# Hybrid encoder block on one core: four of twelve 128-column turns move from TensorE to VectorE blocks and transfers

## The reference

```python
h = rms_norm(x, g_mix);  proj = h @ w_in          # z | xbc | dt | q | k | v | gates
y = ssd_scan_both_ways(conv(xbc), dt) + d_skip * xs
y = rms_norm_by_group(y * silu(z)) * norm_g        # 8 groups of 256 channels
attn = gqa(rope(norm(q)), rope(norm(k)), v)
x = x + (sigmoid(ga) * (y @ w_ssm_up) + sigmoid(gb) * (attn @ w_attn_up)) @ w_out
x = x + relu(rms_norm(x) @ w_mlp_in)**2 @ w_mlp_out
out = rms_norm(x) * g_final
```

## Time and profile before

| | us |
|---|---|
| median of 3 runs (1622.29 to 1622.76) | 1622.51 |
| profiled execution, first to last instruction (its span) | 1620.0 |
| outside of the span, median less span | 2.5 |
| PE busy | 1608.5 (99%) |
| DVE busy | 1264.1 (78%) |
| ACT busy | 917.1 (57%) |

### The profile page before, as it was taken

One profiled execution on the slowest core, in us unless ns is written; L12 is line 12 of the kernel. 1 busy time (PEld: TensorE's weight loads), 2 busy tenths in 40 slices (PEclk: granted clock), 3 DMA queues, 4 the chain that ended last, 5 costly groups with the idle time before them and its releaser, 6 DMA issues.

```text
span 1620.0 us, 20751 instructions
## 1 busy us (share of the span) xinstructions
PE 1608.5 (99%) x8104; PEld 1362.2 (84%) x8104; DVE 1264.1 (78%) x1520; ACT 917.1 (57%) x1262; POOL 79.1 (5%) x67
## 2 busy tenths in 40 slices
PE   9999999999999999999999999999999999999998
PEld 7888888888888888888888888888888888888886
DVE  7888878888666677776665576999799988998893
ACT  6666556666565445544444555665556556655562
POOL 3000000000001134000000000000000000000000
PEclk9999999999999999999999999999999999999999
DMA  7666665666556664445576676458646764586471
GB/s 272 202 200 190 189 200 189 208 195 203 183 186 182 191 187 153 142 145 175 187 229 195 225 236 187 144 182 285 184 125 224 262 190 134 194 282 209 148 245 53
DMA packets 134194, 312.21 MB, mean 193 GB/s; under 512 B 9744, under 2 KB 10448, under 8 KB 133968
## 3 DMA queue, kind: packets, MB, share of 16 engines
q1 hardware_dynamic: 129376, 302.21, 58.4%
q10 hardware_dynamic: 4720, 8.68, 2.0%
HBM read 308.68 MB, written 2.16 MB: 192 GB/s over the span
## 4 chain that ended last, share of the span: by engine, by line
PE 96%; DVE 2%; issue 1%; ACT 0%; POOL 0%; DMA 0%; POOLq 0%; DVEq 0%
PE G L1719 17%; PE G L1720 17%; PE G L1721 17%; PE G L1728 13%; PE S L1728 7%; PE G L1732 6%; PE S L1719 4%; PE S L1721 4%; PE S L1720 4%; PE S L1732 4%; PE S L1740 1%; PE S L1847 1%; DVE wlo L1022 1%; PE S L1891 0%; PE S L1824 0%
## 5 line engine op out<-in xcount | busy, mean ns | idle before, releaser
L637 ACT ACTIVATE whi<-raw 128x1024 fp32r<-128x1024 f32 x395 | 417.0, 1059 | 418.1 <-PE G L1721 254.9
L1022 DVE TENSOR_TENSOR wlo<-raw,whi 128x1024 fp32r<-128x1024 f32 x395 | 482.5, 1236 | 128.7 <-ACT whi L637 127.4
L1719 PE MATMUL G<-whi,a_both 128*128 128x512 f32 x768 | 301.3, 392 | 2.3 <-DVE wlo L1022 1.7
L1721 PE MATMUL G<-whi,a_both 128*128 128x512 f32 x768 | 299.5, 390 | 0.0
L1720 PE MATMUL G<-wlo,a_both 128*128 128x512 f32 x768 | 299.5, 390 | 0.0
L1728 PE MATMUL G<-a_both,whi 128*128 128x512 f32 x640 | 201.7, 397 | 0.0
L1719 PEld LDWEIGHTS G<-whi,a_both 128*128 128x128 f32 x768 | 144.3, 188 | 33.3 <-issue 2.6
L1721 PEld LDWEIGHTS G<-whi,a_both 128*128 128x128 f32 x768 | 144.2, 188 | 30.1
L1720 PEld LDWEIGHTS G<-wlo,a_both 128*128 128x128 f32 x768 | 144.3, 188 | 28.7
L1732 PEld LDWEIGHTS G<-a_both,wlo 128*128 128x128 f32 x640 | 120.3, 188 | 28.2
L1719 PE MATMUL G<-whi,b_hi 128*128 128x512 f32 x342 | 133.9, 392 | 0.0
(11 more groups left out here) (306 smaller groups left out, 2692.4 us busy)
## 6 DMA issues: line engine op xcount, KB each, us to landing
raw<-in_w_in SPq DMA_DIRECT2D x208, 512.0 KB, 4.3
raw<-in_w_mlp_in SPq DMA_DIRECT2D x74, 512.0 KB, 4.0
raw<-in_w_mlp_out SPq DMA_DIRECT2D x74, 512.0 KB, 5.0
gates<-in_w_mlp_in SPq DMA_DIRECT2D x54, 512.0 KB, 4.0
gates<-in_w_mlp_out SPq DMA_DIRECT2D x54, 512.0 KB, 4.9
raw<-in_w_ssm_up SPq DMA_DIRECT2D x32, 512.0 KB, 3.8
raw<-in_w_attn_up SPq DMA_DIRECT2D x32, 512.0 KB, 4.6
raw<-in_w_out SPq DMA_DIRECT2D x32, 512.0 KB, 4.6
```

The lines of the kernel that those rows point to most:

```text
L637: act.activation(high(m), piece(n), ACT.Copy).then_inc(hi_made, 1)
L1022: dve.tensor_tensor(low(m), piece(n), high(m).bitcast(F32), ALU.subtract).then_inc(lo_made, 1)
L1719: pe.matmul(out_ap, hi[:, k, cols], w_hi, start=start, stop=False)
L1721: return pe.matmul(out_ap, lo[:, k, cols], w_hi, start=False, stop=stop)
```

## The change

Rounds 0 to 3 of the turning (the four parts of y) no longer use PE. Instead:

- zgate step 5, DVE: one `transpose` instruction turns each 32 by 32 block of `tmp_a` in place in the grid and writes `blocks` (128 partitions by 1024).
- zgate step 6, ACT: a transfer puts `blocks` into device memory, `block_rows`.
- next window, new side function `zturned`, step 0, ACT: waits until the transfer has landed, and issues four transfers that fetch the blocks to their places in `turned_to`; each goes to 32 partitions, in runs of 32 elements (128 bytes).
- step 3, ACT: waits for all four and writes `b_hi` from `turned_to`; step 4, DVE: writes `b_lo`.

`zturned(j)` stands ahead of `zgate(j + 1)`, and for j = 3 ahead of `rope(0)`. The buffers lie where the scan's tables were. Rounds 4 to 11 stay on PE; their code gains branches that are not taken, and two waits of PE on earlier rounds are placed a few steps apart from before.

```diff
 TS_Z, TS_MERGED, TS_X2, TS_END = 0, 4, 8, 12
+ON_PE = {rnd: i + 1 for i, rnd in enumerate((*range(TS_MERGED, TS_END),))}
+BLOCK_ROUNDS = [rnd for rnd in range(TS_END) if rnd not in ON_PE]
+Q = 32
...
-    window(9, 0, "z", 2, [("zgate", 1)])
-    window(9, 1, "z", 3, [("zgate", 2)])
-    window(10, 0, "k", 0, [("zgate", 3)])
-    window(10, 1, "v", 0, [("rope", 0)])
+    window(9, 0, "z", 2, [("zturned", 0), ("zgate", 1)])
+    window(9, 1, "z", 3, [("zturned", 1), ("zgate", 2)])
+    window(10, 0, "k", 0, [("zturned", 2), ("zgate", 3)])
+    window(10, 1, "v", 0, [("zturned", 3), ("rope", 0)])
...
+        def put_blocks(rnd):
+
+            d = BLOCK_ROUNDS.index(rnd)
+            act.wait_ge(blocks_turned, d + 1)
+            act.dma_start(block_rows[d], blocks[:, :, :].rearrange("p b n -> p (b n)")).then_inc(s_put, 16)
+
+        def get_blocks(rnd):
+
+            d = BLOCK_ROUNDS.index(rnd)
+            act.wait_ge(s_put, 16 * (d + 1))
+            if rnd:
+                act.wait_ge(ts_lo, rnd)
+            rows = block_rows[d].rearrange("(i r) (m j w) -> j r m i w", i=4, j=4, w=Q)
+            for j in range(4):
+                act.dma_start(turned_to[Q * j:Q * (j + 1), :, :].rearrange("r m (i w) -> r m i w", i=4), rows[j]
+                              ).then_inc(s_got, 16)
...
-            act.wait_ge(ts_t, rnd + 1)
+            if rnd in ON_PE:
+                act.wait_ge(ts_t, ON_PE[rnd])
+            else:
+                act.wait_ge(s_got, 64 * (BLOCK_ROUNDS.index(rnd) + 1))
...
-            if p == 7:
+            if p == 6:
+                put_blocks(TS_Z + j)
+
+        def zturned(p, j, pr, pp):
+            if p == 0:
+                get_blocks(TS_Z + j)
+            if p == 3:
                 split_high(TS_Z + j, b_hi, 4 * j, gain=2)
...
+        def turn_blocks(rnd, src):
+
+            d = BLOCK_ROUNDS.index(rnd)
+            if d:
+                dve.wait_ge(s_put, 16 * d)
+            dve.transpose(blocks[:, :, :].rearrange("p b n -> p (b n)").rearrange("p (c b t) -> p c b t", c=4, b=TB),
+                          src.rearrange("p b (c t) -> p c b t", c=4)).then_inc(blocks_turned, 1)
...
-            if p == 7:
+            if p == 5:
+                dve.wait_ge(z_v, (j + 1) * Z_V)
+                turn_blocks(TS_Z + j, tmp_a[:, :, :])
+
+        def zturned(p, j, pr, pp):
+            if p == 4:
                 split_low(TS_Z + j, b_hi, b_lo, 4 * j, gain=2)
...
-        def zgate(p, j, pr, pp):
-            if p == 6:
-                pe.wait_ge(z_v, (j + 1) * Z_V)
-                if j == 0:
-                    pe.wait_ge(scan_v, SCAN_V * GROUPS)
-                split_round(TS_Z + j, lambda c, tb: tmp_a[:, tb, c * P:(c + 1) * P])
-
```

More of the change, by code:

```diff
@@ L543, in build @@
     cum_rows = nc.dram_tensor("cum_rows", (2, HEADS, T), F32).ap()
+    block_rows = nc.dram_tensor("block_rows", (len(BLOCK_ROUNDS), P, TB * N), F32).ap()
+    by_channel = turned_to[:, :, :].rearrange("p (c b) t -> p c (b t)", b=TB)
     block = keep.enter_context(nc.Block())
@@ L654, in split @@
             high_part(m, n)
-        def split_high(rnd, dst, k0, gain=None, factor=1.0):
-            act.wait_ge(ts_t, rnd + 1)
+        def put_blocks(rnd):
[11 more added lines that the diff above has]
+                              ).then_inc(s_got, 16)
+        def split_high(rnd, dst, k0, gain=None, factor=1.0):
+            if rnd in ON_PE:
+                act.wait_ge(ts_t, ON_PE[rnd])
+            else:
+                act.wait_ge(s_got, 64 * (BLOCK_ROUNDS.index(rnd) + 1))
+                if gain is None:
+                    last = act.activation(dst[:, ds(k0, 4), :], by_channel,
+                                          ACT.Copy, scale=factor)
+                else:
+                    for c in range(4):
+                        last = act.activation(dst[:, k0 + c, :], by_channel[:, c, :],
+                                              ACT.Copy, scale=gains[:, gain * KT + k0 + c:gain * KT + k0 + c + 1])
+                last.then_inc(ts_hi, 1)
+                return
             if gain is None:
@@ L831, in zgate @@
                 if j:
-                    act.wait_ge(ts_t, TS_Z + j)
+                    act.wait_ge(blocks_turned, j)
                 else:
@@ L913, in merged @@
         def merged(p, j, pr, pp):
-            if p == 2:
+            if j + TS_MERGED not in ON_PE and p == 1:
+                put_blocks(j + TS_MERGED)
+            if j + TS_MERGED not in ON_PE and p == 3:
+                get_blocks(j + TS_MERGED)
+            if p == (2 if j + TS_MERGED in ON_PE else 6):
                 split_high(j + TS_MERGED, b_hi, j * 4, factor=0.5)
         def residual(p, j, pr, pp):
+            if TS_X2 + j not in ON_PE and p == 1:
+                put_blocks(TS_X2 + j)
+            if TS_X2 + j not in ON_PE and p == 3:
+                get_blocks(TS_X2 + j)
+            if p == (2 if TS_X2 + j in ON_PE else 6):
+                split_high(TS_X2 + j, a_hi, 4 * j, gain=1)
             if p == 2:
-                split_high(TS_X2 + j, a_hi, 4 * j, gain=1)
                 for tb in range(TB):
@@ L977, in finish @@
                     final_squares(j, tb)
-        table = {f.__name__: f for f in (rates, decays, conv, scan, gate, zgate, rope, values, attend, merged,
+        table = {f.__name__: f for f in (rates, decays, conv, scan, gate, zgate, zturned, rope, values, attend, merged,
                                          residual, hidden, finish)}
@@ L1052, in split @@
                 low_part(m, n + i - 3)
+        def turn_blocks(rnd, src):
[4 more added lines that the diff above has]
+                          src.rearrange("p b (c t) -> p c b t", c=4)).then_inc(blocks_turned, 1)
         def split_low(rnd, hi, lo, k0, gain=None, factor=1.0):
             dve.wait_ge(ts_hi, rnd + 1)
+            if rnd not in ON_PE:
+                if gain is None:
+                    part = slice(k0, k0 + 4)
+                    last = dve.scalar_tensor_tensor(
+                        out=lo[:, part, :], in0=by_channel, scalar=factor, in1=hi[:, part, :].bitcast(F32),
+                        op0=ALU.mult, op1=ALU.subtract)
+                else:
+                    for c in range(4):
+                        k = gain * KT + k0 + c
+                        last = dve.scalar_tensor_tensor(
+                            out=lo[:, k0 + c, :], in0=by_channel[:, c, :], scalar=gains[:, k:k + 1],
+                            in1=hi[:, k0 + c, :].bitcast(F32),
+                            op0=ALU.mult, op1=ALU.subtract)
+                last.then_inc(ts_lo, 1)
+                return
             if gain is None:
@@ L1456, in residual @@
                 add_product(j, pr, pp, lambda tb: out_product(j, tb))
-            if p == 2:
+                if TS_X2 + j not in ON_PE:
+                    dve.wait_ge(taken[pp], pr + 1)
+                    turn_blocks(TS_X2 + j, x_sb[:, j, :, :])
+            if p == (2 if TS_X2 + j in ON_PE else 7):
                 split_low(TS_X2 + j, a_hi, a_lo, 4 * j, gain=1)
@@ L1571, in finish @@
                     times_gain(j, tb)
-        table = {f.__name__: f for f in (rates, decays, conv, scan, tables, zgate, rope, attend, gated_a, merged,
+        table = {f.__name__: f for f in (rates, decays, conv, scan, tables, zgate, zturned, rope, attend, gated_a, merged,
                                          residual, hidden, sums, mixed, mix_out, finish)}
@@ L1912, in merged @@
         def merged(p, j, pr, pp):
-            if p == 1:
+            if p == 1 and j + TS_MERGED in ON_PE:
                 pe.wait_ge(merge_v, j + 1)
@@ L1918, in residual @@
         def residual(p, j, pr, pp):
-            if p == 1:
+            if p == 1 and TS_X2 + j in ON_PE:
                 pe.wait_ge(taken[pp], pr + 1)
@@ L1928, in residual @@
                 last.then_inc(row_mm, 1)
-        table = {f.__name__: f for f in (rates, decays, conv, scan, zgate, rope, attend, merged, residual)}
+        table = {f.__name__: f for f in (rates, decays, conv, scan, rope, attend, merged, residual)}
         def last_window(r, par, idx):
@@ L2072, in window @@
                 if p == 0 and rounds is not None:
-                    pe.wait_ge(ready, rounds - 1 if late else rounds)
+                    pe.wait_ge(ready, rounds - 2 if late else rounds)
                 if p == 0 and kind == "mlp_in" and idx[1] == 1:
                     pe.wait_ge(hid_hi, 1)
+                if p == PIECES - 4 and late:
+                    pe.wait_ge(ready, rounds - 1)
                 if p == PIECES - 2 and late:
```

21 lines of the change are left out of this document (15 added, 6 removed).

## The result

The changed kernel takes 1636.7 us (median of 4 runs, 1635.0 to 1637.8) against 1622.5 before: ratio 1.0086, 95% interval 1.0073 to 1.0100. It is slower by 14.2 us. The profiled execution took 1635.0 us with a span of 1633.0, 13.0 above the span before.

What follows compares the result with a forecast made beforehand. PE bounds the kernel, 96% of the chain. PE's waits for late fetches less 3.5 us gained give +10.7 at 20 ns a run, +4.4 at 15; +7.5 makes span 1627.5, median 2.5 above, 1630 us; range 1618.5 to 1645.

Steps and rivals of the forecast that it cites:

- its own last sentence: Sign for the four windows: reason wrong if ACT's time goes to issues or put; forecast wrong if fetches land within 9 us, PE never waiting.
- The gain of 3.5 us: On PE, four turns of y at 0.88 us each go, saving 3.5 us if all of it is kept.
- DVE's turn: One turning instruction of 1024 columns on DVE in each of four windows, taken at 1.2 us, covered even at 2.4.
- The put: 512 KB transfer to device memory, landing 5.7 us after issue; if issued late, ACT stands 2.8 us in the next window.
- The issues: On ACT, four fetch issues at step 0, 0.44 us each, 1.8 us ahead of the product's copies.
- The rival that took this maximum for all four: At step 0, each issue holds ACT 2.02 us, 8.1 for four, so PE waits at step 4; 1639 us, chance 0.13.
- The price of a run: Transfer engine time for one 128-byte run of a fetch, chosen as 15 to 20 ns between bounds of 6.4 and 110.
- the even rates of long packets: 2 KB and 4 KB weight packets show no fixed part above 7 ns, giving 6 to 13 ns a run.
- factor of 19: Skill page's slowdown for a transfer turning by access pattern, against 1309 ns for 128 by 128; carried over as 24 ns a run.
- The sum of 1637 us: Time of the changed kernel if a run costs the 24 ns estimated from the skill page; some 1637 us.
- The late landing: Fetches land after 10 to 14 us, ACT stands before b_hi at step 3, PE waits; 1624 to 1645, chance 0.52.
- the first slack: DVE's low part for step 4 is done at t = 7.25, PE wants it at 10.88; 3.6 us to spare.

Runs made afterwards that it cites:

- two and two: Changed kernel with fetches 0 and 1 issued at step 0, 2 and 3 at step 2, b_hi at step 5, b_lo at 6; 1618.9 us, ratio 0.9979.
- behind the copies: Changed kernel with only the order at step 0 changed: the four issues stand after the copies from the product; 1619.7 us, ratio 0.9990.
- long rows: Changed kernel with each fetch moving 32 whole rows of 4 KB in place of 1024 runs of 128 bytes, output different; 1619.1 us, ratio 0.9980.
- one a step: Changed kernel with one fetch at each of steps 0 to 3, after the product's copies, b_hi at step 6, b_lo at 7; 1618.9 us, ratio 0.9979.
- half: Changed kernel with four fetches of 512 runs of 256 bytes in place of 1024 of 128, output different; 1623.7 us, ratio 1.0004.
- twice: Changed kernel with eight fetches of 1024 runs of 64 bytes, same bytes in all, output different; 1653.0 us, ratio 1.0188.

## Why the prediction was right, and where its reason was not

The direction, slower, was right, and +14.2 us lies in the range, in its upper part, against +7.5 forecast. The reason was not: the forecast had PE waiting because the fetches land late; PE waited because the issues hold ACT ahead of the copies. By its own last sentence ("its reason is wrong if ACT's time goes to the issues") the mechanism failed, and that the number lies in the range is luck.

- **The gain of 3.5 us** was right: the three kernels without PE's turns of y and with nothing blocked came out at ratios of 0.9979 and 0.9980, 3.3 to 3.5 us.
- **DVE's turn** at 1.2 us was right (1.24), and covered.
- **The put**: forecast 5.7 us, measured 3.9 to 6.3. The 2.8 us that ACT was to stand for a late put in the windows behind the first did not come: in z 3 the put landed at 473.55 by the chain, and ACT's first high part ended at 473.84.
- **The issues were the step that failed**: "four at step 0, 0.44 us each by the median ... 1.8 us ahead of the product's copies". They took 5.1, 8.1, 4.3 and 7.6. The row this came from the earlier trace rows was of transfers of 256 packets, at most two at a time; what it could not show was room running out. Nor did its maximum of 2.02 us: that is one issue of 16 in the trace before, the same issues take at most 0.50 in seven of the other nine traces (1.56 and 1.95 in two), and what held it is not known. The rival that took this maximum for all four, at 1639 us, had the right place and a chance of 0.13. Its size was near by luck: the measured issues are not alike, the first two take 0.6 to 1.0 and the third 2.2 to 4.4.
- **The price of a run** was forecast at 15 to 20 ns, with 6 to 13 from the even rates of long packets. From the page's queue rows (before):

```profile
q10 hardware_dynamic: 21936, 12.87, 3.1%
```

  the added time is 0.031 x 16 x 1633 - 0.020 x 16 x 1620 = 292 us; less 512 packets of the puts at 0.21, 184 us for 16384 runs, 11 ns. The shares are rounded, and the same reckoning gives 9 to 14 ns in the profiles of "two and two" (3.0% of 1616.5) and "behind the copies" (3.3% of 1616.9), so 11 is good to 2 or 3. The value lies inside the 6 to 13 ns of the even rates, which I had set aside for a choice without a row (bytes alone are 6.6 there, not 6.4; nothing hangs on it). The page of the Trainium skill (VectorE: DVE Perf Modes, The three transpose paths) gives its factor of 19 for a copy whose innermost destination stride is large; to carry it over to whole runs of 128 bytes was my step, and the 24 ns that came of it do not agree with this row. The sum of 1637 us worked out from it hit the time by chance, through a wait that was another one.
- **The late landing** did not happen in these windows. The fetches landed 3.7 to 8.0 us after their issue, against 10 to 14 forecast. The last fetch of z 2 was issued at 453.87, and ACT took `b_hi` at 462.91 straight behind its other work. Since ACT was held by the issues, it came to that place late itself.
- **Where PE waits**: the first slack of 3.6 us, worked out for step 4, was the right quantity. Issues of 5.13 and 8.06 less 3.6 give 1.5 and 4.5; the trace has 1.54 and 4.31. For the window k, 4.27 less 3.6 gives 0.7, and the trace has 0.19. For the fourth window the rival had about 6; the three waits there are 1.48, 1.21 and 3.24.

The sum of the profiled execution: waits 8.7 + 3.2 = 11.9, about 0.3 at each of six for what the wait's row leaves out 1.6 (a matmul that starts behind a wait is followed 0.1 late, and the row counts the wait from the modelled end, 0.16 after the next could have started), clock 2.2, waits elsewhere 0.6, turns -3.5: 12.8 of the 13.0 measured. The forecast had nothing for the clock. The profiled execution is the fastest of the four; the 1.7 us that the median lies above it are in no profile.

**Settled**: the cost is issues of short runs that wait, ahead of the copies (long rows, two and two, one a step, behind the copies), and it grows with the number of runs (half, twice). That they wait for room is the reading that fits all these rows, the end of the third issue just ahead of the first landing above all; no run looks at the queue itself. **Open**: where the room is was not tried, nor whether fetches issued from another engine's queue have room of their own. Why the windows z 3 and v have the long issues is open too. Full transfer engines do not explain it, since the window k (third row) is as full and has the shortest issues, 4.27 us:

```profile
450.10:455.30 5.20, 5.20 (x25) 4.30 (x24) 1.23 (x1) 0.14 (x1) 0.00 (x0) 1.00 0.84 223
473.60:481.60 8.00, 8.00 (x37) 6.60 (x37) 1.23 (x1) 0.24 (x1) 0.00 (x0) 1.00 1.04 278
501.90:506.30 4.40, 4.40 (x21) 3.64 (x20) 1.23 (x1) 0.66 (x1) 0.00 (x0) 1.00 1.04 288
```

## What to carry to other kernels

The duration of a transfer's issue in a trace is its price at the place where it was measured; here it said nothing of four issues of many short runs in a row. Before several transfers of many short runs are issued in a row, count the runs for each of the 16 engines; here 128 were issued with little or no standing, and with more the issuing engine stood for 2 to 4 us at the third transfer, with all its own work behind it. Spread such issues over the steps, and put them behind the instructions that others wait for: the same transfers cost 17.8 us together at the head of a step (1636.7 against 1618.9) and nothing that these runs could tell one at a time.

## What the runs showed of the hardware

- A run of 64, 128 or 256 bytes from device memory takes about 10, 11 and 19 ns of a transfer engine (estimates, the same reckoning from the queue rows: 38576 packets at 3.6% of a span of 1650.1 and 13744 at 3.0% of 1624.8; for 128 bytes 9 to 14 over the runs), and a 4 KB packet 0.21 us by the prediction's estimate.
- Two transfers of 64 runs for each engine are issued in about 0.6 and 0.7 to 1.0 us; a third right behind them takes 1.4 to 4.4 (runs of 128 bytes). Pairs about 5 us apart, or single ones 2 to 3 us apart, take 0.56 to 1.2 each in the windows z 2 to v.
- One `transpose` of 128 by 1024 float32 in blocks of 32 by 32 takes DVE 1.24 us.
- One wait of PE of 4.3 us was followed by 5 us at half the granted clock; waits of 1.2 to 3.2 us in the same trace were not. In the run with half the runs a wait of 2.7 us was followed by about 3 us at half.
